# One more pair of hidden tiles by seven block products in a decoder layer's MLP

## The reference, cut to what matters

```
x = x + merged @ w_out
h2 = rms_norm(x, g_mlp)
x = x + square(relu(h2 @ w_up)) @ w_down      # w_up 1024 x 4096, w_down 4096 x 1024
```

## Time and profile before

| | |
|---|---|
| runs shown | 1001.07, 1000.27, 999.69 us; median 1000.27 |
| the profiled execution's own time | 998.83 us |
| its span in the trace | 997.1 us |
| mean granted PE clock | 0.989 |
| PE busy | 963.9 us, 7506 matmuls |
| DVE busy | 596.4 us |
| ACT busy | 440.7 us |
| from device memory and back | 99.86 MB, mean 100 GB/s |

### The profile page before, as it was taken

How to read it: one execution, slowest core, us unless ns; L and a number is a source line. 1 busy time by engine, 2 the same in 40 slices (tenths; PEclk the granted TensorE clock), 3 DMA queues, 4 the chain that set the end, 5 groups by cost and what they waited for, 6 DMA issues and landing times.

```text
span 997.1 us, 17803 instructions
## 1 busy us (share of the span) xinstructions
PE 963.9 (97%) x7506; PEld 924.4 (93%) x7506; DVE 596.4 (60%) x803; ACT 440.7 (44%) x663; POOL 62.6 (6%) x111
## 2 busy tenths in 40 slices
PE   5799999999999989999999999999999999999998
PEld 4698989998888879999999999999999999999997
DVE  6278769922354552446556856666667666777543
ACT  6233424233455563453435654444444444445532
POOL 5000011410100032010000000000000000000000
PEclk9989999999899999999999999999999999999999
DMA  9252214741551119443222222222222222242202
GB/s 206 26 146 64 85 35 126 133 146 50 157 167 65 55 51 364 145 159 85 80 80 74 86 84 86 85 86 85 85 85 86 85 85 85 86 141 78 80 1 96
DMA packets 139969, 99.86 MB, mean 100 GB/s; under 512 B 24401, under 2 KB 130193, under 8 KB 139857
## 3 DMA queue, kind: packets, MB, share of 16 engines
q1 hardware_dynamic: 133344, 81.02, 28.4%
q0 software_dynamic: 5424, 17.65, 5.8%
q10 hardware_dynamic: 1120, 0.04, 0.1%
HBM read 87.54 MB, written 11.03 MB: 99 GB/s over the span
## 4 chain that ended last, share of the span: by engine, by line
PE 89%; SPq 4%; ACT 3%; issue 2%; DVE 1%; DMA 1%; ACTq 0%
PE dense L2011 60%; PE banks L2011 19%; PE scoreA L2011 4%; PE scoreB L2011 3%; PE banks L2141 3%; SPq L889 3%; SPq L869 1%; DMA cnat<-in_ssm_c_im 1%; ACT whi L1139 0%; PE dense L2141 0%; DVE mt L1581 0%; ACT ga L1452 0%; DVE mt L1507 0%; ACT yh L1459 0%; SPq L874 0%
## 5 line engine op out<-in xcount | busy, mean ns | idle before, releaser
L1531 DVE TENSOR_TENSOR wlo<-wraw,whi 128x1024 fp32r<-128x1024 f32 (+1 forms) x139 | 148.6, 1072 | 75.3 <-ACT whi L1139 62.9
L2011 PE MATMUL dense<-hid,whi 128*128 128x288 f32 x1024 | 178.7, 297 | 0.0
L2011 PE MATMUL dense<-act_hi,whi 128*128 128x288 f32 (+2 forms) x736 | 165.9, 307 | 1.7 <-DVE R L1608 0.9
L2011 PE MATMUL dense<-act_hi,wlo 128*128 128x288 f32 (+2 forms) x736 | 160.0, 299 | 0.0
L2011 PE MATMUL dense<-act_lo,whi 128*128 128x288 f32 (+2 forms) x736 | 159.2, 297 | 0.0
L2011 PEld LDWEIGHTS dense<-hid,whi 128*128 128x128 f32 x1024 | 150.2, 188 | 0.3 <-issue 0.2
L2011 PEld LDWEIGHTS dense<-act_hi,whi 128*128 128x128 f32 x736 | 119.7, 193 | 8.6 <-issue 5.3
L1139 ACT CAST whi<-wraw 128x1024 fp32r<-128x1024 f32 x100 | 104.9, 1050 | 45.6 <-PE banks L2011 44.2
L2011 PEld LDWEIGHTS dense<-act_hi,wlo 128*128 128x128 f32 x736 | 119.9, 191 | 0.0
L2011 PEld LDWEIGHTS dense<-act_lo,whi 128*128 128x128 f32 x736 | 118.8, 190 | 0.0
L2011 PE MATMUL dense<-hid,wlo 128*128 128x288 f32 x512 | 110.1, 296 | 0.0
(11 more groups left out here) (339 smaller groups left out, 1561.2 us busy)
## 6 DMA issues: line engine op xcount, KB each, us to landing
wraw<-in_w_in SPq DMA_DIRECT2D x32, 512.0 KB, 4.7
wraw<-in_w_up SPq DMA_DIRECT2D x32, 512.0 KB, 4.1
wraw<-in_w_down SPq DMA_DIRECT2D x32, 512.0 KB, 3.8
gates_spill<-gst POOLq DMA_DIRECT2D x16, 288.0 KB, 2.4
page<-in_cache_k SPq DMA_DIRECT2D x16, 256.0 KB, 3.6
page<-in_cache_v SPq DMA_DIRECT2D x16, 256.0 KB, 5.7
wraw<-in_w_out SPq DMA_DIRECT2D x8, 512.0 KB, 4.0
wraw<-in_w_ple_gate SPq DMA_DIRECT2D x8, 512.0 KB, 4.0
```

Source lines behind the costliest of these rows:

```text
L1531: return nc.vector.tensor_tensor(out=lo, in0=whole, in1=f32(hi), op=ALU.subtract)
L2011: return nc.tensor.matmul(out, lhsT, rhs, start=start, stop=stop, skip_group_check=True)
```

## The change

FIRSTPAIR goes from 6 to 4. Hidden tiles 4 and 5, until now two up units, become one more pair, which stands directly behind up 3; the down units 0 and 2 follow it instead of standing between up 4, up 5 and the first pair. The four xpair and four xsplit events now stand between up 0 and the first pair, so xsplit 3 is directly ahead of it. Of the eight rscale events one stands ahead of up 3; the others are done inside the first two pairs, one ahead of each of their products 0 to 2 and 0 to 3. A pair now takes a list of these tiles. The number of pairs (NPAIR) goes from 13 to 14, and the general loop starts at tile 8.

```diff
--- before.py
+++ after.py
@@ -91,7 +91,7 @@
 
 
 DENSE = 4
-FIRSTPAIR = 6
+FIRSTPAIR = 4
 NPAIR = (32 - FIRSTPAIR) // 2
 LASTHID = 28
 LASTCUT = ((0, 256), (256, T))
@@ -161,10 +161,12 @@
                 dense_job(("m", n[0], j))
             n[0] += 1
 
-    def pair():
+    def pair(scaled=()):
 
         u, m = n[0], units[n[0]][1]
         for j in range(7):
+            if j < len(scaled):
+                event("rscale", scaled[j])
             flush()
             if j == 6:
                 event("hid", m, 0)
@@ -388,27 +390,19 @@
     event("ms", 0)
     event("msinv", 0)
     event("xpair", 1)
-    event("rscale", 0)
-    event("rscale", 4)
     unit()
     event("xsplit", 0)
-    event("rscale", 1)
-    event("rscale", 5)
+    event("xpair", 2)
     unit()
-    event("xpair", 2)
     event("xsplit", 1)
+    event("xpair", 3)
+    event("rscale", 0)
     unit()
-    event("xpair", 3)
     event("xsplit", 2)
-    event("rscale", 2)
-    unit()
     event("xsplit", 3)
-    event("rscale", 3)
-    unit()
-    event("rscale", 6)
-    event("rscale", 7)
-    unit(2)
-    for m in range(FIRSTPAIR, 32, 2):
+    pair(scaled=(1, 2, 3))
+    pair(scaled=(4, 5, 6, 7))
+    for m in range(FIRSTPAIR + 4, 32, 2):
         if m == LASTHID - 8:
             event("inv")
         pair()
```

## The result

The changed kernel takes 1009.36 us, the median of five runs (1006.62 to 1010.49), against 1001.07 us before (999.69 to 1002.81, five runs): 1.0078 times as long, 95% interval [1.0058, 1.0099]. It is slower, beyond what can be told from no change.

What follows compares the result with a forecast made beforehand. The prediction took PE, busy 97% of the span, to bound the kernel. Its terms, -1.60 - 1.14 + 8.93 + 2.3 = +8.5 us, added to the median 1000.27, gave 1008.8 us, range 1005 to 1011.5.

Steps and rivals of the forecast that it cites:

- The gains: Up 4, up 5 and first pair: twelve matmuls fewer, 1.60 us, and no wait before up 5, 1.14 us.
- The standstill: Ahead of the first pair: PE waits 8.93 us for the low parts of all four xt tiles.
- The walk's sequence: ACT and DVE queues traced event by event from xsplit 0; first product starts at about 564.95 instead of 556.02.
- The walk's lower bound: Ahead of the first pair: DVE's 16.5 us of work alone makes at least 6.5 us of standstill.
- The clock: Behind the standstill: PE runs at granted clock 0.50 for a while, costing 2.3 us (ends 1.5 and 3.0).
- What is hidden: First pair and pair 6: later blocks and rscales cost PE nothing; pair 6 cover thin, some 0.6 us.
- The sum: Whole kernel: -1.60 - 1.14 + 8.93 + 2.3 = +8.5 us, giving 1008.8.
- One sign that I named: Profile after: about 9 us PE idle ahead of the first pair, released by the low part of XT.
- the one in which the sums are ready in time: Rival at the first product: no wait for low parts, only the gain of 2.74 us, 997.5; chance 0.04.
- The clock did not hold: Rival behind the standstill: standstill as walked but no slow stretch, +6.2, 1006.5; chance 0.08.
- no second wait came behind the first: Rival: PE also waits within pair 4 or 6, or handovers cost more; 1011.0; chance 0.15.
- DVE did wait on ACT: Judges the rival ahead of the first pair that DVE never waits on ACT: 6.5 us standstill, 1006.3; chance 0.13.

Runs made afterwards that it cites:

- e7: Changed kernel with sums begun earlier, XT wait at product 1, block 3 prepared behind product 0, blocks 4 to 6 behind product 1; 0.9969 of the kernel before.
- e6: Kernel before (first pair at tile 6) with the activation sums prepared earlier and the rscales in twos behind later units; 0.9988 of the kernel before.
- e5: Kernel before with rscale 3 moved one unit later, behind down 0; 0.9997 of the kernel before.
- e3: Changed kernel with 64 unused matmuls into a free bank ahead of the wait for XT; 1.0067 of the kernel before.
- e1: Changed kernel with the wait for the four XT low parts moved from product 0 to product 1; 1.0074 of the kernel before.
- e4: Changed kernel with activation sums begun earlier, rscale 0 and mean square later, and the XT wait at product 1; 0.9991 of the kernel before.
- e2: Changed kernel with weight blocks 2 and 3 prepared behind xsplit 3 instead of ahead of up 3's outputs; 1.0041 of the kernel before.

## Why the prediction was right

Forecast 1008.8, measured 1009.36. That the two lie so close is in part luck: the forecast added 8.5 to a median of 1000.27, the runs of the kernel before measured with the change had 1001.07, and the interval on the difference is +5.8 to +9.9 us. The norm-to-norm distance tests the steps more finely:

- **The gains**, 1.60 for the matmuls and 1.14 for the wait at up 5: e7 shows their sum (2.76 against 2.74). Separately e6 and e7 give 0.88 for the order and 1.88 for the rest, so the 1.14 was the right sum of what is lost there. The reason was incomplete: e5 shows that 0.80 of it hung on a single rscale in DVE's queue, not on up 5.
- **The standstill**: walked 8.93, measured 9.34. The walk's sequence holds: ACT waits for a wsum (2.7 walked, 2.91 measured), the ReLU of up 3 is 2.9 late by the walk and 3.3 in the trace. Of the 0.4 too little, 0.27 came from handovers: the xpairs on DVE started 0.13 and 0.14 us after the end of the XT low part ahead of them (549.35 + 1.36 to 550.84, and 556.98 + 1.36 to 558.48, in the changed kernel's timeline of DVE), where I let them start with the end. The walk's lower bound, DVE's load alone, was 6.5 us; the 2.05 us in which DVE waited for ACT are most of what lies between.

```profile
549.35 1.36 DVE L1525 TENSOR_TENSOR XT<-xt,XT 128x1152 fp32r<-128x1152 f32 x1 [0.30 <-ACT XT L1287]
550.84 0.83 DVE L1501 TENSOR_TENSOR xt<-xu 128x288 f32<-128x288 f32 x2
...
556.98 1.36 DVE L1525 TENSOR_TENSOR XT<-xt,XT 128x1152 fp32r<-128x1152 f32 x1 [0.30 <-ACT XT L1287]
558.48 0.83 DVE L1501 TENSOR_TENSOR xt<-xu 128x288 f32<-128x288 f32 x2
```

- **The clock**: 2.3 us put in, from a slow stretch of 5.2; measured 4.6 us at 0.50, 2.1 us by the same 45%, and 2.04 by e3. The Trainium skill's reckoning of half the slow stretch ("TensorE: Matmul & The Clock Gate", section "Terms") would give an estimate of 2.3; e3 is nearer to the 45%. The reason given for expecting a slow stretch, "three of three gaps of this kind", was chosen from more: in the same trace PE stood idle for 1.96 us ahead of 15.69 and 1.37 us ahead of 19.03, and the clock stayed at 1.00 from 12 to 22 us, while the stretch from 261.20 came behind idle times of only 1.29 and 0.67 us. A standstill of 9 us is nearest to the gap of 7.5 us ahead of 50.9, which the forecast took.
- **What is hidden**: in the changed kernel's pair 6 the four rscales end at 600.04 and DVE's next turn is at 600.89, 0.84 us of cover where I had 0.6. No wait there:

```profile
598.50 1.54 DVE L1501 TENSOR_TENSOR R<-R,msq 128x576 f32<-128x576 f32 x2
600.89 0.46 DVE L1501 TENSOR_TENSOR hr<-psave,banks 128x288 f32<-128x288 f32 x1 [0.84 <-PE banks L2005]
```

- **The sum**: -1.60 - 1.14 + 9.34 + 2.1 is +8.7, and +8.74 is measured from norm to norm; +8.3 between the medians. The forecast's +8.5 has the standstill 0.4 too short and the clock 0.2 too dear, two errors that half cancel.
- One sign that I named was wrong: the releaser shown is "issue", not the low part of XT. e1 gives the name, with the wait for XT moved to product 1.
- **Of the rivals**, the one in which the sums are ready in time was false for this order. But e4 shows that the reason against it (16.5 us of DVE's work do not fit into 9.4) was about the order and not about the work: in the changed kernel DVE is idle for 2.80 us just ahead of 548.28, and with the sums begun one unit sooner, sums and blocks fit. The clock did not hold; no second wait came behind the first; and DVE did wait on ACT.

## What to carry to other kernels

A step that needs fewer matmuls has a deadline for its preparation that moves forward with it. Count the preparing engines' load up to that deadline, and walk their queues as well. Here DVE's load was most of the standstill, and a cast that waited for DVE, with a ReLU and two XT casts queued behind it, added about 2 us; together with the clock they turned a saving of 2.7 us into a loss of 8.7. The same work, begun one unit sooner and put in another order, gave the saving in full. And when a wait goes, look at once for who is behind it in the queue: e4 removed nine microseconds of waiting and met 2.3 at the next bank. An idle time of PE can cost more than itself: 2.0 us more behind the 9.3 us of the changed kernel, 1.6 more behind the 2.3 us of e4, nothing behind the 1.07 us of the kernel before.

## What the runs showed of the hardware

An idle time of 2.2 us was followed by a low granted clock in e4 (0.52 over 3.55 us; 0.50 is 1.2 GHz). In the gap ahead of up 5 in the kernel before, 0.91 us idle, the clock stayed at 1.00. No safe length follows from these two. At the start of the kernel PE is idle twice shortly after one another. In the kernel before this was 1.96 and 1.37 us, at 1.00 throughout. In e7 it was 1.97 and 2.23 us, and there the clock was 0.52 from 17 to 22 us. And behind 1.29 and 0.67 us (258.82 and 260.12 in the kernel before) the clock was 0.50 from 261.20 on.

The clock also falls in one execution and not in another at the same place in unchanged code. The part ahead of the MLP, 2.75 us longer in the changed kernel's profile, has such a place, while the kernel before shows 1.00 over the same time:

```profile
226.00:227.00 1.00, 1.00 (x9) 0.50 0.00 0
228.00:230.00 2.00, 2.00 (x10) 0.50 0.00 0
232.00:234.00 2.00, 2.00 (x21) 1.00 0.80 228
```

```profile
220.00:240.00 20.00, 19.18 (x165) 1.00 0.24 79
```

(columns here: length, PE busy and its matmuls, granted clock, DMA share, GB/s). The matmuls of the state-space output around it, in the kernel before and in the changed one (count, lengths in ns, first and last start):

```profile
L2011 PE MATMUL banks<-UT,Tm x64: 226/275/330, 205.6 to 234.9; 128*128 128x72 f32 x64
```

```profile
L2005 PE MATMUL banks<-UT,Tm x64: 226/275/487, 204.1 to 236.4; 128*128 128x72 f32 x64
```

They take 29.3 us in the one and 32.3 in the other. e2 and e3 have the low clock at this place too, the other five experiments do not. Such a stretch makes single spans differ by 3 us for no reason in the code, which is more than most effects studied here. The distance between two marks around the change did better: as a difference (from the changed kernel for e1 to e3, from the kernel before for e5 to e7) it agreed with the expectation to 0.3 us or better in all experiments but e4, whose second wait the walk had missed. Why the clock falls at that place in some executions only stays open; nothing was tried on it.
